# A transformer-style trunk layer: the last block of pass B gathers its expert rows instead of multiplying the whole second table

## The chip, the cores and the metric

The kernel runs on one core of a Trainium2 chip. A core has TensorE (matrix products), VectorE (DVE), ScalarE (ACT) and GpSimd (POOL), SyncE (SP) which here only issues transfers, and 16 DMA engines that all queues share. The metric is the time of one execution on the device in microseconds. The kernel before takes 2957.24 us, the median of three runs (2951.74 to 2960.56).

## The reference

x is 1024 tokens of 1024 features, eight blocks of 128 tokens, all float32.

```
h   = LN(x) * (1 + scale1) + shift1
[u, v, gB, gC, z, ga, gb] = h @ W_in
yA  = gelu(u) * (W_s . LN(gelu(v)) + b)         yB = gB * conv3(gC * z)
m   = sigmoid(ga) * (yA @ P_A) + sigmoid(gb) * (yB @ P_B)
x   = LN(alpha * x + gate1 * (m @ W_o))
h2  = LN(x) * (1 + scale2) + shift2
x   = LN(alpha * x + gate2 * PEER(h2))
```

PEER is where the change lies. Each token forms 8 queries (heads); each is scored against two sets of 128 keys; the 16 best pairs of keys name 16 of 128 x 128 = 16384 experts, with softmax gates. An expert is one row of `expert_u` and one of `expert_v` (1024 values each): the token's result is the sum over its 8 x 16 = 128 experts of gate x gelu(u_row . h2) x v_row.

## The kernel before, in words

**Two passes.** Pass A holds blocks 0 to 2, pass B blocks 3 to 7 (`NBLK`, line 39). `UNITS` (`_order`, line 54) is one list of work units that every engine goes through in the same order: the front layers of A, those of B with A's queries among them, then B's queries among its first E units, 64 E units, and 64 W units, two W units to a group. A unit is 1 MB of weights. Products are made exact enough in fp16: weights and activations are each split into a high and a low half, and three matmuls (high x high, high x low, low x high; lines 1718 to 1720) stand for one. ScalarE makes the high half of a unit's weights (`make_hi`), VectorE the low half (`make_lo`, line 1043), three or four units ahead (`NW` = 4 slots, two staging buffers).

**Pass A is sparse.** Its experts' rows are gathered: 384 slots (3 blocks x 128), for each slot one row of either table for 128 tokens at once, 4096 bytes a token. GpSimd issues one indirect transfer for a slot (line 746) once the row buffer is free (`row_used`), VectorE dots a first-table row with h2 (`u_row`, line 1139) or adds a weighted second-table row (`v_row`, line 1148). `SECTION` says how many slots of each table go beside which unit, `_places` gives each row a buffer out of the ring of its phase (`BUFFERS`: 7 buffers beside the ranking, 5 and 6 around the spreading, 9 in the main loop).

**Pass B is dense.** For all 16384 experts the E units compute gelu(u_row . h2) for the 640 tokens (96 matmuls of 320 columns a unit) and store them, `a_dram`. VectorE meanwhile ranks the scores of B head by head (`rank`). In the spread units, 20 from unit 40 on, 32 tokens a unit, the gates are spread out to a dense table of experts by tokens: VectorE builds one-hot matrices (`onehot_keys`, line 1496, `onehot_gate`, line 1503), TensorE multiplies them, ScalarE stores the result, `g_dram`. Four E units follow them.

**The main loop.** 32 groups of 512 experts. SP loads a group's activations (`A_t`) and every second time two groups' gates (`G_t`); VectorE multiplies them (`product`, line 1510), ScalarE makes the high half, VectorE the low one (`coefficients_lo`, line 1519). TensorE multiplies these coefficients with the group's second-table rows: 10 output tiles, five blocks by two halves of the features, 12 matmuls of 512 columns each. Seven tiles stay in seven banks of PSUM over all groups. The other three share the eighth bank, and VectorE adds them into SBUF after each group (`shared_out`, line 1641). Pass A's rows go on beside it: 5 or 6 slots of each table a group up to group 23, then those of the second table alone.

**The end.** When the last product is made, SP loads the residual blocks back (`x_end`), and VectorE and ScalarE close one block after another in `CLOSE_ORDER`: scale, add, layer norm, store.

The queues run in the order in which the program is written; there is no planner. On VectorE an iteration of the main loop is:

```
some(1)
make_lo(first_w + 2 * g + NW - 1)
shared_out(g, 0)
product(g + 1)
some(2)
shared_out(g, 1)
coefficients_lo(g + 1)
make_lo(first_w + 2 * g + NW)
some(2)
```

Of the kernel before, what the change touches and what calls it, by code (L numbers as in the profile page):

```python
# [175 lines left out]
X_G = X_IDX + 6  # L176
X_END = X_G + NT // 4
# [13 lines left out]
N_SPREAD = NT // 32  # L191
E_SPREAD = 2 * NGRP - N_SPREAD - 4
# [8 lines left out]
SLOTS = SB * HEADS * TOPK  # L201
LAG = 32


def _sections():
# [6 lines left out]
    for e in range(2 * NGRP):  # L212
        k["B", "E", e] = 2 + e % 2 if e < E_SPREAD - 4 else 2
# [25 lines left out]
ROW_OF = {row[:2]: m for m, row in enumerate(ROWS)}  # L239

# [4 lines left out]
           "out": [0, 1, 2, 3, 12, 13, 14, 15, 16]}  # L245
# [38 lines left out]
SHARED = ((1, 0), (4, 0), (2, 1))  # L284
OUT_ORDER = [(b, half) for half in range(2) for b in range(DB)]
# [4 lines left out]
FINISH = [((0, 0), (N_MAIN,)), ((0, 1), (N_MAIN,)), ((1, 1), (N_MAIN,)), ((0, 0), (N_MAIN + 1,)),  # L290
          ((0, 1), (N_MAIN + 1,)), ((1, 0), (N_MAIN, N_MAIN + 1)), ((1, 1), (N_MAIN + 1,))]
FINISH += [((b, half), (N_MAIN, N_MAIN + 1)) for b in range(2, DB) for half in range(2)]
FINISHED = {t: i + 1 for i, (t, _) in enumerate(FINISH)}
LAST_SHARED = [t for t, _ in FINISH if t in SHARED]
CLOSE_ORDER = [0, 1, 3, 4, 2, 5, 6, 7]
SHARED_POS = [OUT_ORDER.index(t) for t in SHARED]

# [1730 lines left out]
```

## Time and profile before

| | us |
|---|---|
| median of three runs | 2957.24 |
| span of the profiled execution, first to last instruction | 2939.3 |
| TensorE busy | 2830.0 |
| VectorE busy | 2512.5 |
| GpSimd busy | 1029.0 |
| ScalarE busy | 885.5 |

The page gives only the span of the profiled execution; the median lies 17.9 us above it. A busy share is a mean over stages with different limits. The granted clock of TensorE was 0.99 of full speed over the span. A matmul's duration in a row (381 ns for 512 columns) contains its pipeline; they start closer together than that. "Idle" in a group's row is the engine's idle time just before its instructions, with what ended it. The share of DMA is the mean over the 16 engines of the time in which packets were under way.

### The profile page before, as it was taken

How to read it: one execution, taken by the hardware profiler on the slowest of the kernel's cores; microseconds unless marked ns; L12 is line 12 of the kernel's file. 1: busy time of each engine (PE TensorE's matmuls, PEld its weight loads, DVE VectorE, ACT ScalarE, POOL GpSimd, SP SyncE). 2: the span in 40 equal slices, each digit the busy share in tenths (PEclk: the TensorE clock that was granted, in tenths of full speed). 3: DMA queues.
4: the chain of work that ended last, by engine and by line, in shares of the span. 5: the costliest groups of instructions: out<-in, count | busy, mean ns of one | idle time of the engine just before them, and what ended most of it. 6: DMA issues, size and time to landing. Idle time of an engine off the chain costs nothing. (4 is left out here: it accounts for less than half of the span.)

```text
span 2939.3 us, 47358 instructions
## 1 busy us (share of the span) xinstructions
PE 2830.0 (96%) x19184; PEld 1834.9 (62%) x19184; DVE 2512.5 (85%) x4708; ACT 885.5 (30%) x1321; POOL 1029.0 (35%) x778
## 2 busy tenths in 40 slices
PE   4999999998999999999999999999999999999998
PEld 4566686766667877677776677777544444444443
DVE  6876556987887879999999999998699999999877
ACT  3333532221111432222222344444222222222223
POOL 0000000002776025444554532222456566655410
PEclk9999999999999999999999999999999999999999
DMA  8989653433999458888888999999999999999972
GB/s 328 348 318 381 238 199 129 144 123 115 391 392 378 192 215 288 303 325 314 330 315 320 354 327 346 350 346 341 368 398 405 405 388 414 407 401 404 364 267 115
DMA packets 222971, 917.54 MB, mean 312 GB/s; under 512 B 20208, under 2 KB 61216, under 8 KB 181536
## 3 DMA queue, kind: packets, MB, share of 16 engines
q1 hardware_dynamic: 61664, 427.91, 37.3%
q0 software_dynamic: 110592, 402.70, 36.4%
q10 hardware_dynamic: 50496, 83.89, 7.9%
q8 instruction: 152, 2.49, 0.3%
q14 instruction: 67, 0.55, 0.1%
HBM read 771.79 MB, written 142.63 MB: 311 GB/s over the span
## 5 line engine op out<-in xcount | busy, mean ns | idle before, releaser
L1718 PE MATMUL psU<-hB,w 128*128 128x320 f16 (+2 forms) x3104 | 927.4, 299 | 27.4 <-ACT Z L753 15.9
L1719 PE MATMUL psU<-hB,w 128*128 128x320 f16 (+2 forms) x3104 | 927.3, 299 | 0.0
L1720 PE MATMUL psU<-hB,w 128*128 128x320 f16 (+2 forms) x3104 | 927.0, 299 | 0.0
L753 ACT ACTIVATE w<-stage 128x2048 f16<-128x2048 f32 x176 | 335.7, 1909 | 606.1 <-PE psX L1720 331.2
L1043 DVE SCALAR_TENSOR_TENSOR w<-stage,w 128x2048 f16<-128x2048 f32 x176 | 402.3, 2287 | 99.4 <-ACT w L753 99.4
L746 POOL DMA_INDIRECT rows<-in_u_rows,idx_sp x200 | 267.8, 1339 | 376.0 <-DVE rows L1139 233.5
L1718 PEld LDWEIGHTS psU<-hB,w 128*128 128x128 f16 x3104 | 304.9, 98 | 140.2 <-issue 22.9
L1720 PEld LDWEIGHTS psU<-hB,w 128*128 128x128 f16 x3104 | 305.1, 98 | 117.6
L1719 PEld LDWEIGHTS psU<-hB,w 128*128 128x128 f16 x3104 | 305.0, 98 | 110.4
L746 POOL DMA_INDIRECT rows<-in_v_rows,idx_sp x205 | 271.4, 1324 | 285.4 <-DVE rows L1139 184.5
L1718 PE MATMUL psX<-w,Z 128*128 128x512 f16 x768 | 292.2, 381 | 7.6 <-DVE Z L1641 4.2
L1719 PE MATMUL psX<-w,Z 128*128 128x512 f16 x768 | 292.6, 381 | 0.0
L1720 PE MATMUL psX<-w,Z 128*128 128x512 f16 x768 | 292.5, 381 | 0.0
L1148 DVE SCALAR_TENSOR_TENSOR acc_sp<-rows,weight_sp,acc_sp 128x1024 f32<-128x1024 f32 x205 | 258.3, 1288 | 30.5 <-DMA rows<-in_v_rows,idx_sp 26.2
L1718 PE MATMUL psU<-w,Z 128*128 128x512 f16 (+1 forms) x768 | 265.1, 345 | 5.4 <-ACT acc_sp L753 2.8
L1139 DVE SCALAR_TENSOR_TENSOR rows<-rows,h_sp 128x1024 f32<-128x1024 f32 x200 | 239.6, 1220 | 29.8 <-DMA rows<-in_u_rows,idx_sp 28.9
L1719 PE MATMUL psU<-w,Z 128*128 128x512 f16 (+1 forms) x768 | 265.1, 345 | 0.0
L1720 PE MATMUL psU<-w,Z 128*128 128x512 f16 (+1 forms) x768 | 265.0, 345 | 0.0
L753 ACT ACTIVATE R<-psU 128x320 f32<-128x320 f32 (+1 forms) x296 | 123.1, 427 | 333.6 <-PE psU L1720 333.3
L753 ACT ACTIVATE Z<-psU 128x320 f32<-128x320 f32 (+3 forms) x228 | 97.0, 445 | 383.6 <-PE psU L1720 341.6
L1718 PE MATMUL psU<-Z,w 128*128 128x384 f16 (+1 forms) x640 | 206.5, 323 | 5.6 <-DVE w L1043 5.6
L1720 PE MATMUL psU<-Z,w 128*128 128x384 f16 (+1 forms) x640 | 206.8, 323 | 0.0
(263 smaller groups left out, 4435.8 us busy)
## 6 DMA issues: line engine op xcount, KB each, us to landing
stage<-in_u_units SPq DMA_DIRECT2D x64, 1024.0 KB, 8.8
stage<-in_v_units SPq DMA_DIRECT2D x64, 1024.0 KB, 8.0
stage<-in_w_front SPq DMA_DIRECT2D x48, 1024.0 KB, 8.6
hl_dram<-w SPq DMA_DIRECT2D x48, 1024.0 KB, 6.5
w<-hl_dram SPq DMA_DIRECT2D x48, 1024.0 KB, 7.2
a_dram<-R ACTq DMA_DIRECT2D x64, 640.0 KB, 8.0
g_dram<-Z ACTq DMA_DIRECT2D x20, 2048.0 KB, 10.7
Z<-a_dram SPq DMA_DIRECT2D x32, 1280.0 KB, 11.8
```

The costliest lines, as they stand in the source:

```text
L746: pool.indirect_dma_start(row_at[r], None, u_rows if table == "u" else v_rows, bass.IndirectOffsetOnAxis(ap=idx_sp[:, slot:slot + 1], axis ...
L753: return nc.scalar.activation(dst, src, func, scale=scale)
L1043: V.scalar_tensor_tensor(w[:, n % NW, 1, :], stage[:, v % 2, :], WS, w[:, n % NW, 0, :], ALU.mult, ALU.subtract).then_inc(lo_done, 1)
L1139: V.scalar_tensor_tensor(row_at[r], row_at[r], 1.0, h2_sp[:, slot % SB, :], ALU.mult, ALU.mult, accum_out=dots[:, c % 8, j:j + 1]).then_in ...
L1148: V.scalar_tensor_tensor(dst, row_at[r], weight_sp[:, slot:slot + 1], dst, ALU.mult, ALU.add).then_inc(row_used, 1)
L1718: mm(ps, lhs[0](k), rhs[0](k), start=start and s == 0, stop=False)
L1719: mm(ps, lhs[0](k), rhs[1](k), start=False, stop=False)
L1720: last = mm(ps, lhs[1](k), rhs[0](k), start=False, stop=stop and s == n - 1)
```

## The change

The last block of pass B (block 7) still goes through the dense E units, but its second half becomes sparse like pass A: its 128 slots' activations are fetched one value a token out of `a_dram`, by an index made on VectorE (`slots_x`), and its 128 rows of the second table are gathered and added on VectorE (`x_row`). Four blocks instead of five are spread and multiplied: 16 spread units instead of 20, eight E units after them instead of four, 8 output tiles instead of 10, each in a bank of its own, so that nothing is shared. Pass A's slots are dealt out anew: 3 or 4 a unit instead of 2 or 3 in E units 0 to 35, four instead of two in units 36 to 39, two as before in spread units, five instead of two in the last eight, and three or four instead of five or six in the main loop. There the rows of the last block are put between them, from the third group on, 28 batches of four or five; the activations of a batch are fetched two groups ahead of its rows, in one piece, by GpSimd. Cut to its core:

```diff
--- before
+++ after
 NT = NTOK["B"]
 HB = NT // 2
+DV = DB - 1
+NV = DV * P
+LAST_B = NB - 1
...
-N_SPREAD = NT // 32
-E_SPREAD = 2 * NGRP - N_SPREAD - 4
+N_SPREAD = NV // 32
+E_SPREAD = 2 * NGRP - N_SPREAD - 8
...
 SLOTS = SB * HEADS * TOPK
+X_SLOTS = HEADS * TOPK
 LAG = 32
+X_LAG = 2
...
-        k["B", "E", e] = 2 + e % 2 if e < E_SPREAD - 4 else 2
+        k["B", "E", e] = 3 + e % 2 if e < E_SPREAD - 4 else 4 if e < E_SPREAD else 2 if e < E_SPREAD + N_SPREAD else 5
...
+FIRST_W = SEC_OF["B", "W", 0]
+N_BATCH = len(SEC_UNITS) - FIRST_W - X_LAG
+BATCH = [range(X_SLOTS * i // N_BATCH, X_SLOTS * (i + 1) // N_BATCH) for i in range(N_BATCH)]
+
+def batch_of(c):
+    return c - FIRST_W - X_LAG

 def _rows():
     rows = []
     for c in range(len(SEC_UNITS)):
-        rows += [("u", s, c) for s in SEC_U[c]] + [("v", s, c) for s in SEC_V[c]]
+        here = [("u", s, c) for s in SEC_U[c]] + [("v", s, c) for s in SEC_V[c]]
+        last = [("x", s, c) for s in BATCH[batch_of(c)]] if batch_of(c) >= 0 else []
+        while here or last:
+            rows += here[:1] + last[:1]
+            here, last = here[1:], last[1:]
     return rows
...
-           "out": [0, 1, 2, 3, 12, 13, 14, 15, 16]}
+           "out": [0, 1, 2, 3, 8, 9, 12, 13, 14, 15, 16]}
...
-SHARED = ((1, 0), (4, 0), (2, 1))
-OUT_ORDER = [(b, half) for half in range(2) for b in range(DB)]
+OUT_ORDER = [(b, half) for half in range(2) for b in range(DV)]
...
+FINISH = [((b, half), (g,)) for g in (N_MAIN, N_MAIN + 1) for b in range(2) for half in range(2)]
+FINISH += [((b, half), (N_MAIN, N_MAIN + 1)) for b in range(2, DV) for half in range(2)]
...
-CLOSE_ORDER = [0, 1, 3, 4, 2, 5, 6, 7]
+CLOSE_ORDER = [0, 1, 2, LAST_B, 3, 4, 5, 6]
...
-        ps_out = psU + psX[0:3]
-        ps_shared = psX[3]
+        ps_out = psU + psX
...
-        a_dram = nc.dram_tensor("a_dram", [NGRP, P, 4, NT], F32).ap()
-        g_dram = nc.dram_tensor("g_dram", [NGRP // 2, P, NT // 32, 2 * P], F32).ap()
+        a_flat = nc.dram_tensor("a_dram", [NGRP * P * 4 * NT, 1], F32).ap()
+        a_dram = a_flat.rearrange("(g p j t) o -> g p j (t o)", g=NGRP, p=P, j=4)
+        g_dram = nc.dram_tensor("g_dram", [NGRP // 2, P, NV // 32, 2 * P], F32).ap()
...
-                sp.dma_start(A_t[g % 2], a_dram[g]).then_inc(a_in[g % 2], 16)
+                sp.dma_start(A_t[g % 2], a_dram[g][:, :, 0:NV]).then_inc(a_in[g % 2], 16)
...
+            def last_activations(i):
+                if i == 0:
+                    pool.wait_ge(x_slots_ready, 1)
+                for slot in BATCH[i]:
+                    pool.indirect_dma_start(act_x[:, slot:slot + 1], None, a_flat,
+                                            bass.IndirectOffsetOnAxis(ap=at_x[:, slot:slot + 1], axis=0)
+                                            ).then_inc(act_x_in[i], 16)
...
+                if m in FIRST_ROW and 0 <= c - FIRST_W < N_BATCH:
+                    last_activations(c - FIRST_W)
                 if before is not None:
                     pool.wait_ge(row_used, before + 1)
+                at = idx_x if table == "x" else idx_sp
...
+            def x_row(slot, c):
+                r, _, uses = PLACES[ROW_OF["x", slot]]
+                dve.wait_ge(row_in[r], 16 * (uses + 1))
+                dve.wait_ge(weight_x_ready, batch_of(c) + 1)
+                if slot:
+                    dve.wait_ge(row_used, ROW_OF["x", slot - 1] + 1)
+                V.scalar_tensor_tensor(acc_x, row_at[r], weight_x[:, slot:slot + 1], acc_x, ALU.mult, ALU.add
+                                       ).then_inc(row_used, 1)
+
+            def weigh_x(i):
+                dve.wait_ge(act_x_in[i], 16 * len(BATCH[i]))
+                at = slice(BATCH[i][0], BATCH[i][-1] + 1)
+                V.tensor_tensor(weight_x[:, at], act_x[:, at], gate_x[:, at], ALU.mult).then_inc(weight_x_ready, 1)
...
+            def slots_x():
+                i1, i2, gate = (t["B"][:, DB - 1].rearrange("p h k -> p (h k)") for t in (i1_all, i2_all, s_all))
+                low = act_x.bitcast(U32)
+                step(V.scalar_tensor_tensor(weight_x, i1, float(NKEYS), i2, ALU.mult, ALU.add))
+                step(V.tensor_copy(low, i2))
...
+                step(V.tensor_scalar(gate_x, gate, WS * AS, None, ALU.mult))
+                V.tensor_copy(at_x, weight_x).then_inc(x_slots_ready, 1)
...
             for g in range(N_MAIN):
...
                 make_lo(first_w + 2 * g + NW - 1)
-                shared_out(g, 0)
                 product(g + 1)
                 some(2)
-                shared_out(g, 1)
                 coefficients_lo(g + 1)
                 make_lo(first_w + 2 * g + NW)
                 some(2)
                 if g == N_MAIN - 1:
                     product(NGRP - 1)
-                shared_out(g, 2)
...
-                for tile in OUT_ORDER:
-                    if tile in SHARED:
-                        wait(pe, v_free, shared)
-                        shared += 1
-                        out_tile(ps_shared, tile, g, True, True).then_inc(v_ready, 1)
-                    else:
-                        out_tile(ps_out[persistent.index(tile)], tile, g, g == 0, False).then_inc(v_ready, 1)
+                for i, tile in enumerate(OUT_ORDER):
+                    out_tile(ps_out[i], tile, g, g == 0, False).then_inc(v_ready, 1)
```

`CLOSE_ORDER` takes block 7 fourth, out of its own sum `acc_x`. `N_BATCH` is 28. The tiles and views of four blocks are 512 columns wide instead of 640.

## Rows read from the trace of the kernel before

**Rows 1.** The page: span, and busy time of each engine

```profile
span 2939.3 us, 47358 instructions
...
PE 2830.0 (96%) x19184; PEld 1834.9 (62%) x19184; DVE 2512.5 (85%) x4708; ACT 885.5 (30%) x1321; POOL 1029.0 (35%) x778
```

**Rows 2.** Busy time by stretch, with clock, DMA share and GB/s

```profile
core 0: us, PE busy (x) PEld busy (x) DVE busy (x) ACT busy (x) POOL busy (x), PEclk, DMA share, GB/s
1062.00:1251.30 189.30, 184.17 (x1353) 133.47 (x1351) 178.12 (x576) 54.27 (x93) 90.80 (x70) 0.99 0.79 290
1251.30:1573.00 321.70, 321.70 (x2385) 234.32 (x2384) 298.94 (x845) 93.95 (x159) 162.86 (x125) 1.00 0.87 323
1573.00:1711.20 138.20, 125.26 (x928) 90.07 (x927) 130.38 (x286) 44.83 (x74) 68.59 (x51) 0.95 0.85 322
1711.20:2036.00 324.80, 322.18 (x3044) 244.96 (x3042) 319.73 (x453) 149.24 (x267) 86.55 (x76) 1.00 0.96 346
2036.00:2090.00 54.00, 53.28 (x386) 37.45 (x385) 32.60 (x35) 17.91 (x27) 12.40 (x10) 1.00 0.98 384
...
2140.00:2707.60 567.60, 567.60 (x2631) 257.23 (x2630) 544.37 (x599) 135.01 (x88) 347.39 (x239) 1.00 1.01 403
```

**Rows 3.** Instruction groups of 2150 to 2700 us, shapes kept apart

```profile
L746 POOL DMA_INDIRECT R<-in_v_rows,idx_sp x70 | 99.4, 1420 | 39.4 <-issue 17.7 <-DVE R L1139 16.6 <-DVE acc_sp L1148 5.1
L1043 DVE SCALAR_TENSOR_TENSOR w<-stage,w 128x2048 f16<-128x2048 f32 x43 | 98.1, 2283 | 0.0
...
L1519 DVE TENSOR_TENSOR Z<-Z 128x2560 f16<-128x2560 f32 x21 | 59.1, 2813 | 0.0
...
L1641 DVE TENSOR_TENSOR Z<-psX,Z 128x512 f32<-128x512 f32 x64 | 43.7, 683 | 8.4 <-PE psX L1720 8.3
...
L1510 DVE SCALAR_TENSOR_TENSOR Z<-Z,hB 128x640 f32<-128x640 f32 x44 | 33.2, 811 | 0.0
```

**Rows 4.** DMA queues of 2150 to 2700 us: packets, MB, share of 16 engines

```profile
q0 software_dynamic: 33108, 120.58, 55.9%
q1 hardware_dynamic: 10659, 100.41, 44.3%
```

**Rows 5.** VectorE's waits of 2150 to 2700 us

```profile
DVE Z L1641 <- PE psX L1720: 8.3, 9, 1.9
DVE acc_sp L1148 <- DMA R<-in_v_rows,idx_sp: 6.9, 6, 2.5
```

**Rows 6.** VectorE in order of time, one burst of rows in an E unit

```profile
1546.49 1.22 DVE L1139 SCALAR_TENSOR_TENSOR rows<-rows,h_sp 128x1024 f32<-128x1024 f32 x1
...
1547.64 2.48 DVE L1148 SCALAR_TENSOR_TENSOR acc_sp<-rows,weight_sp,acc_sp 128x1024 f32<-128x1024 f32 x2
1550.03 0.16 DVE L1161 SCALAR_TENSOR_TENSOR weight_sp<-dots,gate_sp 128x3 f32<-128x3 f32 x1
```

**Rows 7.** Chain of waits: VectorE's weight conversions of two spread units

```profile
1733.37 2.20 DVE w L1043
...
1750.45 2.20 DVE w L1043
```

**Rows 8.** DMA issues of 1260 to 1600 us: count, KB each, us to landing

```profile
q10 hardware_dynamic: 2880, 13.11, 9.4%
...
rows<-in_v_rows,idx_sp POOLq DMA_INDIRECT x39, 8.2
rows<-in_u_rows,idx_sp POOLq DMA_INDIRECT x33, 9.0
```

**Rows 9.** GpSimd's row issues of 2150 to 2700 us: shortest, median, longest

```profile
L746 POOL DMA_INDIRECT rows<-in_u_rows,idx_sp x55: 933/1438/3044, 2149.9 to 2690.2; - x55
...
DMA to landing us min/median/max: 5.7/10.8/19.1
```

**Rows 10.** VectorE at the end, and its first wait there

```profile
2870.35 3.02 DVE L1510 SCALAR_TENSOR_TENSOR Z<-Z,hB 128x640 f32<-128x640 f32 x4
...
2887.28 1.23 DVE L1674 SCALAR_TENSOR_TENSOR Z<-acc_sp,h_sp 128x1024 f32<-128x1024 f32 x1 [4.93 <-DMA hB<-x_dram]
```

More of the change, by code:

```diff
@@ L239 @@
 ROW_OF = {row[:2]: m for m, row in enumerate(ROWS)}
+ROWS_OF = [[row[:2] for row in ROWS if row[2] == c] for c in range(len(SEC_UNITS))]
+FIRST_ROW = {m for m, row in enumerate(ROWS) if not m or ROWS[m - 1][2] != row[2]}
 BUFFERS = {"front": [0, 1, 2, 3, 4, 5, 6, 7], "own": [0, 1, 2, 3], "rank": [0, 1, 2, 3, 8, 9, 17],
            "gates": [0, 1, 2, 3, 10], "spread": [0, 1, 2, 3, 10, 11], "last": [0, 1, 2, 3, 8, 9],
-           "out": [0, 1, 2, 3, 12, 13, 14, 15, 16]}
+           "out": [0, 1, 2, 3, 8, 9, 12, 13, 14, 15, 16]}
 def _buffers_of(unit):
@@ L489, in trunk_layer @@
         row_in = [sem(f"row_in{i}") for i in range(18)]
+        act_x_in = [sem(f"act_x_in{i}") for i in range(N_BATCH)]
         end_in = sem("end_in")
@@ L828, in indices_out @@
             def indices_out(lo, hi):
-                for i in range(lo, hi):
-                    kind, (first, last) = i // 2, SPLIT["B"][i % 2]
-                    a = X_IDX + i
-                    n, at = (last - first) * P, slice(first * P, last * P)
+                for kind in range(lo, hi):
+                    a = X_IDX + kind
                     wait_x(act, a)
                     if kind < 2:
-                        pairs = slice(first * P // 2, last * P // 2)
-                        activation(keys_t16[:, pairs, kind, :], psX[a % 4][:, 0:n].rearrange("p (n t) -> p n t", t=2)
+                        activation(keys_t16[:, :, kind, :], psX[a % 4][:, 0:NV].rearrange("p (n t) -> p n t", t=2)
                                    ).then_inc(x_free[a % 4], 1)
                     else:
-                        activation(g_t[:, at], psX[a % 4][:, 0:n], ACT.Copy, GS).then_inc(x_free[a % 4], 1)
+                        activation(g_t, psX[a % 4][:, 0:NV], ACT.Copy, GS).then_inc(x_free[a % 4], 1)
             def section_gelu(n):
@@ L1177, in section @@
                         dve.wait_ge(acc_zeroed, 1)
-                for slot in SEC_V[c]:
-                    v_row(slot)
+                for table, slot in ROWS_OF[c]:
+                    if table == "u":
+                        u_row(slot, slot - SEC_U[c][0], c)
+                    elif table == "v":
+                        v_row(slot)
+                    else:
+                        x_row(slot, c)
                     yield
@@ L1480, in idx_t @@
             def idx_t():
-                for i in range(4):
-                    a = X_IDX + 5 - i
+                for a in range(X_IDX, X_G):
                     dve.wait_ge(x_free[a % 4], a // 4 + 1)
@@ L1941, in _ @@
                     pe.wait_ge(s_shift, 2)
-                    index_tiles(0, 4)
+                    index_tiles(0, 2)
             first_w = N_OF["B", "W", 0]
-            persistent = [t for t in OUT_ORDER if t not in SHARED]
             pe.wait_ge(tile_free, E_LAST)
@@ L1949, in _ @@
                 pe.wait_ge(x_free[a % 4], a // 4 + 1)
-            shared = 0
             def out_tile(ps, tile, g, first, last):
```

112 lines of the change are left out of this document (56 added, 56 removed).

## The prediction

> **What bounds the kernel now.** I read the page's busy times first. TensorE is busy 96% of the span and VectorE 85% [rows 1], so an average names no single bound, and I went on by stretches [rows 2]. Up to 1062 us nothing of this change runs. From 1251 to 1573 us (E units, pass B's first-table product with the ranking beside it) TensorE is busy all the time and VectorE 298.9 of 321.7 us: 93%. From 1711 to 2036 us (spread units) VectorE is busy 319.7 of 324.8 us, and two weight conversions a unit apart on the chain of waits stand 17.08 us apart [rows 7]: VectorE is the bound there. From 2036 to 2090 us the last four E units take 13.5 us each and VectorE is busy for only 32.6 of 54.0 us. In the main loop (2140 to 2707 us) TensorE never pauses: 567.6 us for 2631 matmuls is 0.2157 us each, 25.9 us for a group's 120. But in the same stretch VectorE is busy 96%, and the DMA share is 1.01 at 403 GB/s. So three resources stand within a few per cent of each other there, and removing work from TensorE alone tells little. VectorE's waits in it are small (8.3 us on TensorE, 6.9 us on one kind of row) [rows 5]; that only says the rows come just in time.
>
> **What the change does to each resource of a group.** TensorE: 8 output tiles instead of 10, 96 matmuls instead of 120, 96 x 0.2157 = 20.7 us, 5.2 us less. Over 32 groups that would be 166 us, the most the edit could bring.
>
> VectorE: now 544.4 us busy in 21.9 groups, 24.8 us each. Removed: three additions out of the shared bank, 3 x 0.68 = 2.05; four products of 512 instead of 640 columns, 4 x 0.81 x 0.2 = 0.65; the low halves 2048 instead of 2560 wide, 2.81 x 0.2 = 0.56 [rows 3]. Added: one multiplication of weights, 0.16. Rows: now 5.33 dotted and 5.33 added, 10.7 in all. Then, by the sections that the code lays out: groups 0 and 1 have 3 + 3 of pass A; groups 2 to 19 have 3.2 + 3.2 of pass A and 4.6 of the last block, 11.0; groups 20 to 27 have 3.2 added and 4.6 of the last block, 7.8; groups 28 and 29 about 8. So groups 2 to 19 need 24.8 - 2.05 - 0.65 - 0.56 + 0.16 + 0.3 x 1.2 = 22.1 us of VectorE.
>
> DMA engines: 120.58 MB of row gathers are 230 gathers of 0.524 MB and take 55.9% of 550 us, 1.34 us each; SP's loads take 44.3% of 550 us for 100.41 MB, 2.43 us per MB [rows 4]. Check on now: 10.7 x 1.34 + 4.72 MB x 2.43 = 25.8 us a group, what the group takes. After, SP loads 2.10 MB of weights, 1.05 of activations and 1.05 of coefficients: 10.2 us. Groups 2 to 19: 11.0 x 1.34 + 10.2 = 24.9 us. Groups 20 to 27: 7.8 x 1.34 + 10.2 = 20.7 us.
>
> The activation gathers are new: 4.6 a group, 128 descriptors of four bytes each. Nothing like them is in the trace. Below they cost next to nothing (512 bytes), above as much as a row gather with as many descriptors, 1.34 us. I take 0.2 us each, near the low end because a thousandth of the bytes moves, so 0.9 us a group: 25.8 us for groups 2 to 19 and 21.6 us for 20 to 27.
>
> GpSimd issues all of them: 11.0 + 4.6 = 15.6 a group instead of 10.7. An issue is 0.93 us at least, 1.44 us in the median and 3.04 us at worst [rows 9], and 0.30 us lies between two (17.7 us of "issue" before 70 instructions is 0.25, part of them with another wait) [rows 3]. At 1.23 us 15.6 issues take 19.2 us, at the mean of 1.42 + 0.30 they take 26.8 us. The five small gathers go out in one piece, and no freed row buffer is refilled in those 6 to 9 us. I take 26.2 us for groups 2 to 19, a little above the DMA sum and below the GpSimd one, and 21.8 us for 20 to 27.
>
> Sum of the main loop against 25.9 a group: groups 0 and 1 at TensorE's 20.7, -10; groups 2 to 19, 18 x 0.3 = +5; groups 20 to 27, 8 x -4.1 = -33; groups 28 to 31, 4 x -5.2 = -21. At the end VectorE waits for the reload of the residual blocks, which lands 14 us after the last product, and then has eight blocks to close [rows 10]; that chain does not get shorter with TensorE's last two groups, +3. In all **-56 us**. Bounds: -138 if groups 2 to 27 go at VectorE's or TensorE's pace (18 x -3.8, 8 x -5.2), -23 if GpSimd sets 28 us for groups 2 to 19.
>
> On this resource the Trainium skill (DMA: Bandwidth & Descriptors, Specifications) speaks against the change: it puts memory traffic of one core at about 358 GB/s. By that an 11-row group's 9.95 MB would take 27.8 us, 36 us more in all. The trace has 403 GB/s over 568 us, so I go by the trace.
>
> **E units 0 to 39.** The rows taken out of the main loop come here: one more of each table in units 0 to 35, two more in 36 to 39, 44 pairs. In a burst a dotted row starts 1.15 us after the last (1546.49 to 1547.64) and an added one 1.20 us (1547.64 to 1550.03 for two) [rows 6]: 2.35 a pair, 103.4 us of VectorE. Its idle time from 1062 to 1711 us is 11.2 + 22.8 + 7.8 = 41.8 us [rows 2]. Nothing of the ranking goes, as all five blocks are still ranked. If all idle time were filled, the stretch grows by 62 us; if none, by 103. I take that half stays, since part of it is waiting for other engines: **+82 us**. It can be more: bursts become 6 and 8 rows for seven buffers, so the eighth row is asked for only when the first is used, some 8 us before it is needed, and rows land 8.2 to 9.0 us after their issue [rows 8]. In units 38 and 39 eight rows share five buffers.
>
> Building the last block's indices adds a dozen small instructions on a busy VectorE, each like the 0.16 us of [rows 6], with waits between: **+3 us**.
>
> **E units 40 to 63.** Now 20 spread units of 17.08 and four of 13.5, 395.6 us. After, 16 spread units (each still spreads 32 tokens with two rows of each table, so 17.08): 273.3 us. The last eight have ten rows each. VectorE then needs 2.2 + 5 x 2.35 + 0.2 = 14.2 us, TensorE 13.0, but the DMA engines 10 x 1.34 + 1.05 x 2.43 + 0.655 MB x 2.44 (9.4% of 340 us for 13.11 MB [rows 8]) = 17.5 us, and six buffers that turn over in about 0.3 + 9 + 1.2 us give ten rows in 17.5 us too. I take 18, so 144, and 8 more for the first two groups' loads (4.2 MB), which lie today beside the four light units at a DMA share of 0.98 [rows 2]. 425 against 396: **+29 us**. Bounds: -7 (14.5 us a unit, loads hidden) to +45 (20 us).
>
> **Sum.** -56 + 82 + 3 + 29 = +58 us. The profiled execution's span is 2939.3 us; what lies around it, up to the median of 2957.2, is 17.9 us and is not touched. I predict 2957.2 + 58 = **3015 us**.
>
> **Rivals.**
> (a) The transfers are not a bound: DMA share 1.01 is a queue that is kept full, not one that limits, and GpSimd keeps up. For it speaks that TensorE never waits today. Then the main loop gives -138, the last units -7, the E units +72: 2957 - 138 - 7 + 72 + 3 = 2887 us. Against it: the sum of bytes by rate comes out at the group's very time, and the same engines do not exceed 403 GB/s over 568 us. It decides if groups 2 to 19 fall under 24 us.
> (b) The four-byte gathers cost like row gathers, 1.34 us: +6.1 us a group. Groups 2 to 19 then take 31.0 (+92), 20 to 27 take 26.8 (+7), the first two lose most of their gain, and the main loop ends at +78: 3149 us. It is the same count of descriptors that speaks for it, the bytes against it. The Trainium skill (DMA: Bandwidth & Descriptors, Specifications) leans to this side: transfers under 512 bytes are read, modified and written; but the same page's floor of 10.5 ns a packet would make it an estimate of 0.08 us a gather. No row here shows such a gather.
> (c) A wash: the E units fill all of VectorE's idle time (+62), the last eight units run at their DMA sum with the first loads hidden (+17), groups 2 to 19 at 24.9 (-18) and 20 to 27 at 20.7 (-42), -88 with the other terms: 2957 + 62 + 17 + 3 - 88 = 2951 us. Each is possible; all together need transfers without any gap, and they have gaps wherever buffers run out.
>
> **Chances.** Forecast 0.68 (its own range 2980 to 3060), (a) 0.11, (b) 0.07, (c) 0.14, spread from 2930 to 2975. A measurement here tells 0.3%, 9 us. Faster by more: (a) and a third of (c), 0.16. Within: 0.06. Slower: 0.78. The range that leaves out no more than 2 in 10 goes from 2940, into (c), to 3080, short of (b).
>
> **What would show it.** Right: VectorE over 97% busy from 1062 to about 1780 us with TensorE under 95%; spread units still 17.08; the last eight E units at 17 to 19 us with VectorE waiting for rows; groups 2 to 19 near 26 us with TensorE waiting, 20 to 27 near 22. Wrong: groups 2 to 19 at 22 to 23 us (then (a)), above 29 (then (b)), or E units with ranking that grow by less than a pair's 2.35 us minus their share of idle time.

## The result, and the profile after

The changed kernel takes 3035.17 us, the median of four runs (3026.71 to 3036.82), against 2958.03 us of the kernel before on the same chip (2951.74 to 2960.56): the ratio is 1.0262, with an interval of 1.0219 to 1.0305. It is slower, as forecast, by 77 us where 58 were predicted. Its profiled execution took 3035.97 us with a span of 3033.8 us.

The page of the changed kernel, the line of [rows 1] again:

```profile
span 3033.8 us, 45503 instructions
...
PE 2709.3 (89%) x18157; PEld 1756.4 (58%) x18157; DVE 2551.7 (84%) x4713; ACT 844.6 (28%) x1281; POOL 1298.5 (43%) x1035
```

TensorE has lost 120.7 us of work, VectorE has gained 39.2 and GpSimd's issuing 269.5. The one that was relieved is the one whose average was highest; the two others had little room where the change uses them.

To see where the time went, I cut both traces at the same pieces of work: the stores of the activations of E units 1, 38, 41, 56 and 64, and the low halves of the coefficients of groups 2, 20 and 28. The stretches of the changed kernel, in the columns of [rows 2]:

```profile
core 0: us, PE busy (x) PEld busy (x) DVE busy (x) ACT busy (x) POOL busy (x), PEclk, DMA share, GB/s
1101.30:1778.10 676.80, 596.30 (x4218) 421.67 (x4216) 629.72 (x1662) 165.18 (x288) 361.54 (x287) 0.94 0.86 323
1778.10:1864.70 86.60, 46.77 (x352) 33.62 (x350) 74.36 (x103) 16.70 (x30) 51.73 (x41) 0.76 0.87 323
1864.70:2121.10 256.40, 254.33 (x2402) 193.25 (x2400) 252.14 (x357) 117.67 (x211) 68.67 (x61) 1.00 0.97 349
2121.10:2254.70 133.60, 103.75 (x763) 74.31 (x761) 96.73 (x116) 30.16 (x50) 83.00 (x62) 0.90 0.99 375
2254.70:2319.80 65.10, 42.88 (x181) 18.53 (x182) 48.80 (x56) 9.89 (x8) 48.13 (x41) 0.80 0.92 344
2319.80:2754.60 434.80, 394.17 (x1736) 172.58 (x1734) 398.71 (x412) 103.03 (x73) 343.42 (x275) 0.95 1.03 405
2754.60:2921.40 166.80, 162.00 (x743) 72.80 (x742) 153.12 (x136) 45.25 (x28) 131.19 (x102) 0.99 1.02 402
```

The same cuts through the kernel before, for three of them:

```profile
1073.90:1658.10 584.20, 572.78 (x4204) 414.22 (x4202) 548.61 (x1559) 171.77 (x289) 293.04 (x220) 0.99 0.85 314
1658.10:1711.20 53.10, 46.45 (x369) 34.44 (x368) 47.10 (x64) 17.54 (x33) 25.22 (x20) 0.94 0.86 326
2138.40:2605.20 466.80, 466.80 (x2165) 211.49 (x2163) 448.23 (x494) 111.46 (x73) 288.47 (x197) 1.00 1.01 403
```

| stretch | before, us | after, us | difference | predicted |
|---|---|---|---|---|
| up to the first E unit's store | 1073.9 | 1101.3 | +27.4 | 0 |
| E units up to the 38th | 584.2 | 676.8 | +92.6 | } +85 |
| units 39 to 41 | 53.1 | 86.6 | +33.5 | } |
| 15 of the spread units | 256.2 | 256.4 | +0.2 | 0 |
| last eight units (4 spread, 4 light before) | 120.6 | 133.5 | +12.9 | } +19 |
| last unit to the coefficients of group 2 | 50.4 | 65.1 | +14.7 | } |
| groups 2 to 19 (25.93 us each, then 24.15) | 466.8 | 434.8 | -32 | +5 |
| groups 20 to 27 (25.76 us each, then 20.86) | 206.1 | 166.9 | -39 | -33 |
| the rest | 128.1 | 112.4 | -15.7 | -18 |

From the first store on that is +67.0 us against the predicted +58. The 27.4 us ahead of it are code that the change leaves as it was: the kernel before, profiled again, came to its first store at 1095.3 us instead of 1073.9 (run r0_before below). The profile of before was some 16 us shorter than its median: its span of 2939.3 us lies 17.9 us under it, where the spans of the other profiles lie 1.8 to 2.2 us under the time of their own execution. The profile of after stood on its median. So some 16 of the 27.4 us are luck of the one execution. What is left, 11 us, is within what twelve profiles vary there (1068 to 1101 us), and what makes it stays open.

The granted clock of TensorE is lower in the changed kernel (0.952 over the span, 0.990 before). It is the lower of its two levels (1.2 of 2.4 GHz) for short times after TensorE has waited (behind a wait of 8.04 us that ends at 2437.91 us its matmuls take 0.61 us instead of 0.38). That doesn't make TensorE the bound: in groups 2 to 19 its clock is 0.95, by which 96 matmuls of 0.2157 us are an estimate of 21.8 us against 24.15 measured, and it still waits for coefficients:

```profile
PE psU L1775 <- DVE Z L1592: 33.7, 10, 8.0
```

### The profile page after: what moved, and what is told of

It reads as the page before. It is cut to its first block, busy times and chain, and to the rows that moved or that the text cites. A ratio compares the mean times of both kernels' runs of the same rounds, so it can differ in the third digit from the quotient of the medians.

```text
span 3033.8 us, 45503 instructions
## 1 busy us (share of the span) xinstructions
PE 2709.3 (89%) x18157; PEld 1756.4 (58%) x18157; DVE 2551.7 (84%) x4713; ACT 844.6 (28%) x1281; POOL 1298.5 (43%) x1035
## 4 chain that ended last, share of the span: by engine, by line
DVE 33%; issue 20%; DMA 16%; PE 14%; POOL 14%; ACT 2%; SPq 0%; DVEq 0%; ACTq 0%; POOLq 0%
DVE acc_sp L1182 5%; DVE w L1077 5%; PE psU L1775 5%; PE psU L1776 5%; PE psU L1777 5%; POOL rows L783 5%; DMA Z<-in_v_rows,idx_sp 4%; POOL Z L760 4%; DMA rows<-in_v_rows,idx_sp 4%; POOL R L783 3%; DVE Z L1569 3%; DVE rows L1173 3%; POOL Z L783 2%; DMA stage<-in_w_front 2%; DVE Z L1576 2%
## 5 line engine op out<-in xcount | busy, mean ns | idle before, releaser
L1775 PE MATMUL psU<-hB,w 128*128 128x320 f16 (+2 forms) x3104 | 939.7, 303 | 104.1 <-ACT R L790 71.6
L1776 PE MATMUL psU<-hB,w 128*128 128x320 f16 (+2 forms) x3104 | 938.7, 303 | 7.3 <-issue 7.2
L1777 PE MATMUL psU<-hB,w 128*128 128x320 f16 (+2 forms) x3104 | 938.4, 303 | 4.0 <-issue 3.9
L1775 PEld LDWEIGHTS psU<-hB,w 128*128 128x128 f16 x3104 | 308.3, 99 | 226.7 <-issue 105.4
L783 POOL DMA_INDIRECT rows<-in_u_rows,idx_sp x200 | 245.7, 1229 | 328.9 <-DVE rows L1173 196.3
L1777 PEld LDWEIGHTS psU<-hB,w 128*128 128x128 f16 x3104 | 308.4, 99 | 132.8 <-issue 10.6
L1776 PEld LDWEIGHTS psU<-hB,w 128*128 128x128 f16 x3104 | 308.4, 99 | 128.1 <-issue 12.6
L783 POOL DMA_INDIRECT rows<-in_v_rows,idx_sp x222 | 281.6, 1268 | 214.2 <-DVE rows L1173 137.2
L1775 PE MATMUL psU<-w,Z 128*128 128x512 f16 (+1 forms) x768 | 273.4, 356 | 95.4 <-DVE Z L1592 92.4
L1182 DVE SCALAR_TENSOR_TENSOR acc_sp<-rows,weight_sp,acc_sp 128x1024 f32<-128x1024 f32 x222 | 283.5, 1294 | 53.5 <-DMA rows<-in_v_rows,idx_sp 47.1
L1173 DVE SCALAR_TENSOR_TENSOR rows<-rows,h_sp 128x1024 f32<-128x1024 f32 x200 | 238.6, 1222 | 50.1 <-DMA rows<-in_u_rows,idx_sp 37.9
L1776 PE MATMUL psU<-w,Z 128*128 128x512 f16 (+1 forms) x768 | 272.7, 355 | 0.0
L1777 PE MATMUL psU<-w,Z 128*128 128x512 f16 (+1 forms) x768 | 272.3, 355 | 0.0
L790 ACT ACTIVATE Z<-Z 128x2048 f16<-128x2048 f32 (+2 forms) x49 | 81.3, 1675 | 556.8 <-issue 236.4
L783 POOL DMA_INDIRECT Z<-in_v_rows,idx_sp x120 | 153.9, 1282 | 135.8 <-DVE Z L1173 93.0
L1775 PE MATMUL psU<-Z,w 128*128 128x384 f16 (+1 forms) x640 | 206.9, 323 | 3.9 <-DVE w L1077 3.8
L1776 PE MATMUL psU<-Z,w 128*128 128x384 f16 (+1 forms) x640 | 206.8, 323 | 0.4 <-issue 0.4
L1777 PE MATMUL psU<-Z,w 128*128 128x384 f16 (+1 forms) x640 | 206.9, 323 | 0.0
L1777 PE MATMUL psX<-w,Z 128*128 128x512 f16 x512 | 194.8, 381 | 3.1 <-issue 3.1
## 6 DMA issues: line engine op xcount, KB each, us to landing
g_dram<-Z ACTq DMA_DIRECT2D x16, 2048.0 KB, 10.5
```

The source lines that it names most:

```text
L783: pool.indirect_dma_start(row_at[r], None, u_rows if table == "u" else v_rows, bass.IndirectOffsetOnAxis(ap=at[:, slot:slot + 1], axis=0)) ...
L790: return nc.scalar.activation(dst, src, func, scale=scale)
L1173: V.scalar_tensor_tensor(row_at[r], row_at[r], 1.0, h2_sp[:, slot % SB, :], ALU.mult, ALU.mult, accum_out=dots[:, c % 8, j:j + 1]).then_in ...
L1182: V.scalar_tensor_tensor(dst, row_at[r], weight_sp[:, slot:slot + 1], dst, ALU.mult, ALU.add).then_inc(row_used, 1)
L1775: mm(ps, lhs[0](k), rhs[0](k), start=start and s == 0, stop=False)
L1776: mm(ps, lhs[0](k), rhs[1](k), start=False, stop=False)
```

## The experiments

Each ratio is to the kernel before, run on the same chip beside it. Each shortened diff shows what differs from the kernel that is named. Where totals are compared, keep in mind that the part ahead of the first E unit's store, which only the edits of e7 and e8 touch (their gathers begin at about 717 us), took 1068 to 1101 us; so the spans from that store on are given too (1932.5 us in the profile of after).

**r0_before.** The kernel before again, with no edit.

> The kernel before once more, for a second profile. In the changed kernel TensorE lost 27 us between 837 and 1010 us, in units that the change doesn't touch, with gaps of 0.6 to 2.1 us between single matmuls. Theory A (instructions arrive late there, by chance of the execution): this profile may show such gaps too, of any size. Theory B (the change causes it): none here, as in the first profile of before; the first E unit's store is issued at 1074 us again.

Measured: 2967.62 us for the profiled execution, span 2965.8; the other runs of before on that chip went from 2930.59 to 2960.59. The 400 us in mid-front of this profile, and the same 400 us of the first profile of before:

```profile
400.00:800.00 400.00, 376.81 (x2684) 268.77 (x2682) 312.98 (x1066) 90.00 (x165) 69.13 (x56) 0.96 0.48 173
```

```profile
400.00:800.00 400.00, 391.60 (x2880) 286.19 (x2878) 311.87 (x1066) 95.23 (x176) 63.63 (x52) 0.99 0.48 174
```

One code did 2684 matmuls here and 2880 there. Part of the lost time is in gaps of 0.5 to 2.5 us between single matmuls which wait for nothing that the profile shows: from 640 us to the first store 16 gaps and 14.1 us in this execution, 12 gaps and 11.4 us in the profile of after, none in the first profile of before. Another part is the granted clock, which falls to its lower level behind such gaps; 60 us of this profile, and of the first:

```profile
760.00:820.00 60.00, 48.23 (x279) 28.94 (x278) 31.72 (x47) 5.09 (x14) 30.86 (x29) 0.80 0.81 317
```

```profile
760.00:820.00 60.00, 53.52 (x385) 37.91 (x383) 48.62 (x67) 7.27 (x20) 41.56 (x36) 0.94 1.02 404
```

From the first store to the end the two profiles of before agree within 0.3% (1865.4 and 1870.5 us), so the table above can be read from there on, to some 5 us in a stretch (groups 2 to 19 took 26.23 us each in this profile), and nothing ahead of it.

**e1_before_new_deal.** The kernel before, with the changed kernel's deal of pass A's rows: the E units take 44 pairs more and the main loop 88 rows less, but the last block stays dense.

```
-  k["B", "E", e] = 2 + e % 2 if e < E_SPREAD - 4 else 2
+  k["B", "E", e] = 3 + e % 2 if e < E_SPREAD - 4 else 4 if e < E_SPREAD else 2
```

> The kernel before with one part of the change: pass A's slots dealt as 3 or 4 in E units 0 to 35 and 4 in units 36 to 39, the main loop with fewer. Theory A (VectorE sets the pace of E units 0 to 39, and its idle time there is not to be filled): 44 pairs x 2.35 = 103 us, and 10 to 15 us of waits in units 38 to 40, +115; the main loop stays at TensorE's 25.9 us a group, so 3070 us. Theory B (the idle time is filled, what the changed kernel lost comes from its other parts): +62 to +82, 3020 to 3040 us.

Measured: 3076.05 us (3070.11 to 3078.99), ratio 1.0439 (1.0386 to 1.0491). Its E units and its main loop:

```profile
1092.40:1771.10 678.70, 593.07 (x4222) 419.88 (x4220) 629.59 (x1663) 164.39 (x288) 359.93 (x288) 0.94 0.87 323
2276.10:2742.30 466.20, 466.20 (x2162) 211.37 (x2160) 388.71 (x415) 112.62 (x73) 177.29 (x146) 1.00 0.92 351
```

The E units take what they take in the changed kernel (678.7 and 676.8 us), so the deal alone makes this term, and neither the indices nor anything else of the last block. The main loop stays at 25.9 us a group although VectorE has 59.5 us less to do than in the same groups of before (448.2 down to 388.7) and the DMA share falls from 1.01 to 0.92. So TensorE did bind the kernel before; the others were a few per cent behind.

**e2_after_gate_units_light.** The changed kernel, with two rows of each table instead of four in units 36 to 39. In the last two of these only five buffers are to be had.

```
-  ... else 4 if e < E_SPREAD else 2 if e < E_SPREAD + N_SPREAD else 5
+  ... else 2 if e < E_SPREAD + N_SPREAD else 5
```

> The changed kernel with two slots instead of four in E units 36 to 39; the eight pairs go to the main loop. Theory A (eight rows on five buffers make VectorE wait for rows there): the stretch from the 38th to the 41st store falls from 86.6 us by 31 (8 x 2.35 and 12 of waits), the main loop grows by 16 x 1.34 = 21 us, 3025 us. Theory B (the length comes from the last block's indices and the start of the spreading): it falls by 19, 3037 us.

Measured: 3027.13 us (3017.74 to 3028.35), ratio 1.0269 (1.0216 to 1.0321). The stretch from the 38th to the 41st store:

```profile
1774.20:1834.00 59.80, 45.51 (x355) 33.44 (x354) 54.81 (x79) 16.75 (x30) 29.68 (x24) 0.87 0.86 324
```

It gives 26.8 us back, 19.6 us of them VectorE's work (74.4 to 54.8) and 7.2 us its idle time (12.2 to 5.0). The total hardly moves: the eight pairs go to the main loop, where groups 2 to 19 rise from 24.15 to 25.05 us (+16) and groups 20 to 27 from 20.86 to 21.33 (+4). From the first store on it is 1928.0 us against 1932.5. A row costs about the same in either place.

**e3_after_old_deal.** The changed kernel with the old deal: all 44 pairs go back to the main loop.

```
-  k["B", "E", e] = 3 + e % 2 if e < E_SPREAD - 4 else 4 if e < E_SPREAD else ...
+  k["B", "E", e] = 2 + e % 2 if e < E_SPREAD - 4 else ...
```

> The changed kernel with the old deal in E units 0 to 39 (2 or 3, and 2); all 44 pairs go back to the main loop. Theory A (the main loop is bound by the transfers, 1.34 us a row): the E units lose 115 us, the main loop gains 88 x 1.34 = 118, about 3037 us, no better. Theory B (the main loop is bound by VectorE, or has room): at 44 x 2.35 on top of 22.1 us in 20 to 28 groups it grows by less, 40 to 75 us, 2960 to 2995 us.

Measured: 3038.38 us, ratio 1.0317 (1.0236 to 1.0398). Three of the four runs lie between 3021.1 and 3050.8 us, with a median of 3026.0; one took 4684.74 us at a granted clock of 0.56 instead of 0.95, which I can't explain and which nothing here rests on. Its main loop, groups 2 to 19:

```profile
2175.30:2698.30 523.00, 403.25 (x1728) 174.50 (x1728) 462.98 (x493) 102.94 (x73) 413.55 (x327) 0.89 1.01 391
```

The E units are back at 574.4 us, and the groups go up to 29.05 and 25.82 us: 18 x 4.9 + 8 x 5.0 = 128 us more in the loop against 137.6 us less in units 1 to 41. GpSimd makes 327 issues of 1.265 us with 0.30 us after each, 511.7 of the 523.0 us. The deal of the rows is a wash (1926.5 us from the first store on, against 1932.5); what costs is that the changed kernel has the last block's second-table rows and as many small gathers on top.

**e4_no_activation_gathers.** The changed kernel without the four-byte gathers.

```
-  for slot in BATCH[i]:
-      pool.indirect_dma_start(act_x[:, slot:slot + 1], None, a_flat, ...)
...
-  dve.wait_ge(act_x_in[i], 16 * len(BATCH[i]))
```

> The changed kernel without the 128 four-byte gathers of activations (the weights of the last block's rows are then made from other values). In the changed kernel groups 2 to 19 took 24.2 us each. Theory A (GpSimd's issues bind: 275 issues x 1.25 + 0.30 us fill 427 of 435 us): without 4.6 issues a group 7 us of GpSimd go, and the groups fall to VectorE's 22.1 us, the kernel to about 2995 us. Theory B (the DMA engines bind with the bytes of the rows, the small gathers are free on both): 24.0 us a group, 3030 us. Theory C (a four-byte gather holds the DMA engines like a row): 6 us a group less for the DMA engines, which also ends at 22.1 us.

**e5_small_loads.** The changed kernel with the gathers, but SP loads only a quarter of a group's activations from group 2 on, and a sixteenth of the gates from group 4 on.

```
-  sp.dma_start(A_t[g % 2], a_dram[g][:, :, 0:NV])
+  sp.dma_start(A_t[g % 2][:, 0, 0:NV], a_dram[g][:, 0, 0:NV])
...
-  sp.dma_start(G_t[pair % 2] ..., g_dram[pair])
+  sp.dma_start(G_t[pair % 2][:, 0:1] ..., g_dram[pair][:, 0:1])
```

> The changed kernel, but from group 2 on SP loads only a quarter of a group's activations and a sixteenth of its gates (the products then use old values): 1.8 MB a group less, 4.5 us of the DMA engines. Theory A (GpSimd binds): groups 2 to 19 stay near 24 us. Theory B (the DMA engines bind): they fall to VectorE's 22.1 us. If both stand at the same height, 23 to 23.5 us.

**e6_no_gathers_small_loads.** Both edits in one kernel.

> Both of the last two in one kernel: neither the small gathers nor the full loads. Whichever of GpSimd and the DMA engines binds, it is freed: groups 2 to 19 at VectorE's 22.1 us, 20 to 27 at TensorE's 20.7 us, the kernel at about 2990 us. If the groups stay above 23.5 us, what binds is neither (the waits between VectorE and TensorE for the low halves).

Measured, with the main loop of each:

| kernel | median us | ratio (interval) | groups 2 to 19 | 20 to 27 |
|---|---|---|---|---|
| after | 3035.17 | 1.0262 (1.0219 to 1.0305) | 24.15 | 20.86 |
| e4 | 3010.59 | 1.0185 (1.0167 to 1.0203) | 23.69 | 21.01 |
| e5 | 3009.99 | 1.0204 (1.0160 to 1.0248) | 23.68 | 20.56 |
| e6 | 2961.36 | 1.0012 (0.9992 to 1.0032) | 21.96 | 19.79 |

From the first store on the profiles of e4, e5 and e6 took 1916.8, 1917.5 and 1874.2 us: 16, 15 and 58 us less than that of after. What their medians gained beyond that (25, 25 and 74 us in all) lies ahead of it, where nothing was edited.

Stretches of the main loop of e4, of e5, and of e6:

```profile
2300.00:2700.00 400.00, 364.27 (x1635) 160.97 (x1632) 370.96 (x382) 94.72 (x67) 237.54 (x181) 0.96 1.02 411
```

```profile
2300.00:2700.00 400.00, 367.77 (x1652) 162.75 (x1649) 374.16 (x385) 95.59 (x68) 323.16 (x253) 0.97 0.91 336
```

```profile
2300.00:2660.00 360.00, 348.38 (x1608) 156.36 (x1607) 359.32 (x372) 93.75 (x66) 219.39 (x175) 1.00 0.98 370
```

This is the picture of two limits side by side. Without the small gathers GpSimd is free (237.5 us and 181 gaps of 0.3 us make 292 of 400), the DMA share stays at 1.02, and a group gains 0.46 us. Without the bytes the share falls to 0.91, GpSimd is full (323.2 + 253 x 0.3 = 399 of 400), and a group gains 0.47 us. Only with both gone is the next limit reached, and it is VectorE, busy 359.3 of 360.0 us: 21.96 us a group, where the prediction's working had 22.1 for VectorE. A group's time is taken at VectorE's low halves, which can catch up by a group; so the 19.79 us of groups 20 to 27 can lie below TensorE's 20.7. I had expected 2990 us for e6, 29 more than it took; the groups were as expected, so most of the miss is elsewhere: half of it ahead of the first store (1086.3 us against 1101.3), some of it in the first loads (55.1 us from unit 64 to group 2, against 65.1).

In e4 GpSimd waits for row buffers that VectorE has to free. One kind of these waits comes to 96.3 us in the 400 us; in groups 2 to 19 of after all of them made 8.1 us:

```profile
POOL R L779 <- DVE Z L1200: 96.3, 31, 5.1
```

**e7_after_half_rows and e8_before_half_rows.** The kernel after, and the kernel before, with 2048 instead of 4096 bytes gathered for each token and slot; all engines do as much work as with whole rows. The dotted rows are multiplied by zero, so the results are not those of the layer.

```
-  pool.indirect_dma_start(row_at[r], None, u_rows if table == "u" else v_rows, ...)
+  pool.indirect_dma_start(row_at[r][:, 0:512], None, half_rows, ...)
```

> The changed kernel with row gathers of 2048 instead of 4096 bytes a token, at the same count; VectorE works on 1024 columns as before (the other half of a buffer is multiplied by nothing). Theory A (E units 0 to 39 are bound by VectorE's work, and about 35 us of 677 by rows that land late): from the first to the 38th store 640 to 650 us instead of 676.8, and 38th to 41st 75 instead of 86.6 us. Theory B (its idle time there has other causes): no change. Last eight E units: from the 56th to the 64th store 120 instead of 133.5 us. Groups 2 to 19: at VectorE's 22.1 us if the DMA engines bind, near 24 us if GpSimd does.

> The kernel before with row gathers of 2048 instead of 4096 bytes a token, everything else as it is. In the changed kernel this brought 77 us. Theory A (the kernel before is bound by TensorE in the E units and the main loop, by VectorE in the spread units, its transfers only just keep up): the main loop stays at 25.9 us a group, the E units change by less than 5 us, 2950 us in all. Theory B (the transfers bind the main loop before too): its groups fall under 25 us.

Measured: e7 2958.05 us, ratio 1.0001 (0.9988 to 1.0014); e8 2907.36 us, ratio 0.9885 (0.9859 to 0.9910). The E units up to the 38th of e7, then those and the main loop of e8:

```profile
1077.50:1731.30 653.80, 585.01 (x4210) 417.37 (x4208) 628.08 (x1660) 165.21 (x288) 361.94 (x286) 0.95 0.66 221
```

```profile
1068.30:1636.10 567.80, 567.80 (x4204) 412.85 (x4202) 552.05 (x1564) 173.77 (x289) 274.49 (x221) 1.00 0.67 226
2120.00:2680.00 560.00, 560.00 (x2596) 253.81 (x2595) 539.12 (x592) 134.56 (x86) 331.91 (x233) 1.00 0.80 295
```

In e7 groups 2 to 19 stay at 24.15 us with a DMA share near 0.8:

```profile
2250.70:2685.40 434.70, 395.27 (x1747) 173.41 (x1745) 398.75 (x410) 101.77 (x73) 352.13 (x272) 0.96 0.81 288
```

GpSimd alone holds them there: 352.1 + 272 x 0.3 = 433.7 of 434.7 us. That it is the very time of after is chance, as an issue took 1.295 us here and 1.249 there. The gain of e7 is in the E units (-23.0 us) and in the stretches after them (the last eight units take 119.0 instead of 133.5 us), 49 us from the first store on. The rest of the 77 us by which its median is lower lies ahead of that store (1077.5 us instead of 1101.3); no run tells whether the bytes of the rows gathered there have a part in them. In e8 the main loop stays at 25.79 us a group, as expected of a kernel bound by TensorE. I missed the size of the rest: the E units gave 16.4 us, the gate units 6.9 and the handover to the main loop 6.7. So the bytes of the rows already cost the kernel before some 30 us around the E units, which no average of the DMA share (0.85) tells.

**e10_no_last_block.** The changed kernel with nothing of the second table for the last block: neither its gathers nor its added rows, while the product is still 8 tiles.

```
-  BATCH = [range(X_SLOTS * i // N_BATCH, X_SLOTS * (i + 1) // N_BATCH) for i in range(N_BATCH)]
+  BATCH = [range(0) for i in range(N_BATCH)]
...
-  if batch_of(c) >= 0: weigh_x(batch_of(c))
```

> The changed kernel without the last block's second half: neither its activation gathers nor its 128 rows, nor the work on them. Theory A (the last block's sparse path costs what it holds of the queues): groups 2 to 19 are left with 6.4 rows, 18.8 us of the DMA engines, 12 us of GpSimd and 16 of VectorE, so TensorE's 20.7 us bind; 27 us less of E units do not come back. The kernel about 3035 - 18 x 3.4 - 5 = 2965 us, no faster than before although it computes less. Theory B (the new waits between VectorE and TensorE hold the groups, whatever the rows): above 22 us a group.

Measured: 2932.43 us, ratio 0.9971 (0.9959 to 0.9984). A stretch of its main loop:

```profile
2250.00:2600.00 350.00, 346.40 (x1605) 156.71 (x1604) 290.40 (x304) 96.50 (x66) 164.32 (x118) 1.00 0.98 378
```

Groups 2 to 19 take 20.2 us and groups 20 to 27 take 20.73; TensorE binds. The total is lower than I expected, by some 30 us. This profile came to its first store at 1074.6 us instead of 1101.3, which is most of that; from there on it took 1856.2 us, where the kernel before took 1865.4 and 1870.5. The run is a bound for the whole idea: with the E units dealt as they are now, even a last block that costs nothing would gain 0.3% on the kernel before.

No version run here is both complete and faster than the kernel before. Three things were not tried: one indirect transfer that fetches the activations of several slots, E units with more buffers, and a deal between the old and the new one.

## Why the prediction was right, and where its sizes were wrong

The direction and its reason held: three resources stood within a few per cent of each other, and the change takes work from one of them and gives it to the other two and to GpSimd. But that the sum is so close (+67.0 against +58) is luck: two errors of some 40 us cancel. Of its own signs of being right, the spread units (17.09 us) held; VectorE was to be over 97% busy up to 1780 us and was 93%, groups 2 to 19 were to be near 26 us and the last eight E units at 17 to 19 us, and they were at 24.15 and 16.7.

**E units 0 to 39: the mis-sized term.** Predicted +85 with the indices, measured 92.6 + 33.5 = +126.1. The work was right: VectorE is busy 108.4 us more (81.1 and 27.3), and 44 pairs of 2.35 us and the indices make 106. What failed is the step "I take that half stays" for the idle time. Nothing of it was filled; it grew, from 35.6 to 47.1 us up to unit 38 and from 6.0 to 12.2 us after that. VectorE of the changed kernel, in order of time, in one unit beside the ranking:

```profile
1482.76 1.23 DVE L1173 SCALAR_TENSOR_TENSOR rows<-rows,h_sp 128x1024 f32<-128x1024 f32 x1 [0.29 <-DMA rows<-in_u_rows,idx_sp]
...
1488.55 1.22 DVE L1173 SCALAR_TENSOR_TENSOR rows<-rows,h_sp 128x1024 f32<-128x1024 f32 x1 [4.56 <-DMA rows<-in_u_rows,idx_sp]
...
1492.48 1.23 DVE L1173 SCALAR_TENSOR_TENSOR rows<-rows,h_sp 128x1024 f32<-128x1024 f32 x1 [2.70 <-DMA rows<-in_u_rows,idx_sp]
...
1494.27 3.84 DVE L1182 SCALAR_TENSOR_TENSOR acc_sp<-Z,weight_sp,acc_sp 128x1024 f32<-128x1024 f32 x3 [0.55 <-DMA Z<-in_v_rows,idx_sp]
```

and the DMA engines around it:

```profile
1485.00:1500.00 15.00, 12.55 (x81) 8.34 (x79) 8.20 (x9) 3.31 (x6) 6.37 (x6) 0.89 1.02 417
```

VectorE stands idle for nearly half of these 15 us because the rows it is to work on are not there, while the DMA engines are full at 417 GB/s. The mean share of the stretch is 0.86. The waits for rows make most of the idle time, in the changed kernel 33.7 of 47.1 us (the four lines below) and in the kernel before 24.1 of 35.6:

```profile
DVE acc_sp L1182 <- DMA Z<-in_v_rows,idx_sp: 10.9, 4, 4.7
DVE acc_sp L1182 <- DMA rows<-in_v_rows,idx_sp: 9.5, 6, 3.3
DVE rows L1173 <- DMA rows<-in_u_rows,idx_sp: 7.5, 3, 4.6
DVE Z L1173 <- DMA Z<-in_u_rows,idx_sp: 5.8, 2, 3.7
```

Time spent waiting for rows can't be filled with more rows. With half the bytes the waits for rows fall to 15.3 us in e7 and to 0.4 in e8, and the idle time to 25.7 and 15.8. My warning on units 38 and 39 (eight rows, five buffers) was right in kind: idle time there doubles. Which share of the waits is due to the buffers and which to the bytes beyond these runs stays open.

**The main loop, groups 2 to 19.** Predicted 26.2 us, measured 24.15; 18 groups make 37 us. The failed step is "I take 0.2 us each" for the four-byte gathers on the DMA engines, and the margin put on GpSimd. The DMA queues of the 434.8 us, in the columns of [rows 4]:

```profile
q0 software_dynamic: 30263, 101.15, 59.1%
q1 hardware_dynamic: 15865, 74.83, 43.3%
```

Queue 0 moved 101.15 MB, 193 row gathers, in 59.1% of 434.8 = 257 us: 1.33 us each, where [rows 4] gave 1.34, with the 81 small gathers in the same 257 us. Of these 257 us the packets of 4096 bytes took 253.2, and the smaller ones that the trace has 3.9, so a small gather costs the DMA engines about 0.05 us instead of 0.2. On GpSimd each costs an issue like any other:

```profile
L760 POOL DMA_INDIRECT Z<-a_dram,Z x81: 940/1897/2016, 2332.5 to 2753.5; - x81
```

and GpSimd's idle time in this stretch is the 0.3 us between two issues, hardly ever a wait for a buffer:

```profile
POOL R L783 <- issue: 26.9, 83, 1.8
...
POOL Z L760 <- issue: 24.7, 81, 0.3
...
POOL R L783 <- DVE Z L1204: 5.3, 4, 2.9
```

275 issues of 1.249 us and 0.30 us each make 426 of 434.8 us. The mean of an issue was lower than the 1.42 us that I took from [rows 3]. So GpSimd and the DMA engines bind together, the first at 23.7 and the second at 24.7 by its shares, which reach 1.03. The mechanism, an issue's price on GpSimd beside the bytes on the DMA engines, was in the prediction; both came out smaller.

The chain of waits shows how it looks when GpSimd sets the pace, with five small gathers in one piece:

```profile
2405.84 1.68 POOL R L783
2407.52 0.31 issue
2407.82 1.92 POOL Z L760
2409.74 0.30 issue
2410.04 1.90 POOL Z L760
2411.95 0.30 issue
2412.25 2.02 POOL Z L760
...
2417.15 1.78 POOL R L783
```

**Groups 20 to 27** at 20.86 us: predicted 21.8. The DMA sum of 21.6 less the 0.9 that the small gathers don't cost is 20.7, but TensorE's 96 matmuls make 20.7 too, and e10, bound by TensorE, has 20.73 there. e4 has 21.01 and e5 20.56. Which of the two binds these groups stays open.

**Units 40 to 63 and the handover.** The spread units are 17.09 us apart as [rows 7] has them (predicted 17.08). Of the last eight units and the first loads I expected +29, and -10 from groups 0 and 1; together the trace has 0.2 + 12.9 + 14.7 = +27.8 against +19. Up to the store of unit 64 the units cost less than thought (133.5 us), and the handover more: TensorE is busy 42.9 of 65.1 us there. Groups 0 and 1 did not run at TensorE's pace.

**The rivals.** (a), the transfers are no bound: refuted by its own point of decision, groups at 24.15 and not under 24 us, though narrowly, and by e5, where fewer bytes bring 0.47 us a group, and e6. Yet half of its ground was true, as TensorE did bind the kernel before (e1, e8). (b), small gathers priced like row gathers on the DMA engines: refuted by queue 0. Its estimate of 0.08 us a gather spreads 128 packets of 10.5 ns over 16 engines. The Trainium skill (DMA: Bandwidth & Descriptors, Measured) gives that floor as the time of a whole transfer of 64 packets over their number, so by it 128 packets would be an estimate of 1.34 us, the price of (b). The trace has 0.05 us. (c), the wash: its loop was near (24.9 and 20.7 expected, 24.15 and 20.86 measured), but it needed the idle time of the E units filled, and the opposite happened.

The Trainium skill (DMA: Bandwidth & Descriptors, Specifications) puts memory traffic of one core at about 358 GB/s, half of what a stack gives its two cores. By that 175.98 MB would need 492 us; the trace has them in 434.8 us at 405 GB/s, so for this kernel, which runs on one core, that half is no limit and the measurement decides.

## What to carry to other kernels

When several resources are within a few per cent of each other, write down what each needs after the change, work and issue slots alike; relief for one is worth only the distance to the next (here 25.9 to 24.15 us a group, not to 20.7). Idle time that an engine spends waiting for data is no room for more work on data of the same kind: look at what ends it before counting on it. And when taking away either of two costs gives little, take away both in one run before calling them harmless: from the first store on e4 gave 16 us, e5 15 us, both together 58.

## What the runs showed of the hardware that I had not expected

**A gather of four bytes a partition** costs the DMA engines about 0.05 us (above) and GpSimd no less than one of 4096 bytes: 0.94 us at least, where those have 0.93. In groups 2 to 19 the mean is 1.49 us for the 81 small ones and 1.16 us for the 193 others, because the small ones go out in one piece beside VectorE's low halves more often (next point).

**An issue stretches beside VectorE.** An indirect transfer's issue takes 0.93 us, but when it starts while VectorE makes a weight's low half it ends only after that. So it was for all 35 such issues of groups 2 to 19, which end 0.81 to 0.83 us after the low half, and for the 18 that started in a low half of coefficients. GpSimd and VectorE of the changed kernel in order of time:

```profile
2437.78 2.28 DVE L1077 SCALAR_TENSOR_TENSOR w<-stage,w 128x2048 f16<-128x2048 f32 x1
2438.97 1.90 POOL L760 DMA_INDIRECT Z<-a_dram,Z  x1 [0.30 <-issue]
...
2441.18 0.95 POOL L783 DMA_INDIRECT R<-in_u_rows,idx_sp  x1 [0.30 <-issue]
```

The low half ends at 2440.06, the issue at 2440.87, 0.81 us after it; the next issue starts together with the dot of a row (L1173) and takes 0.95 us. Beside such shorter instructions issues took 0.93 to 2.02 us. The Trainium skill (SBUF — State Buffer, Who interferes with whom) says that a VectorE instruction with two inputs in SBUF contends with a GpSimd instruction that reads SBUF, and that the ports they share are locked for one of them. The same section of the Trainium skill infers that making descriptors needs only the write side, by which these issues would not wait. The trace agrees with the first and speaks against the second, as the issues end behind both kinds of low half; the other way round no stretch was seen (the 36 low halves of the loop take 2.28 us in the mean, [rows 3] has 2.28).

**Matmuls that wait for nothing shown.** Some executions reach the first E unit's store 21 to 27 us later than the first profile of before (1095.3 and 1101.3 against 1073.9 us), with 11 to 14 us in gaps of 0.5 to 2.5 us between matmuls, between about 730 and 985 us, and a granted clock at the lower level behind them. One such place in the profile of after, TensorE alone:

```profile
846.29 0.10 PEld L1776 LDWEIGHTS psU<-hB,w 128*128 128x128 f16 x1 [1.74 <-issue]
846.31 0.44 PE L1776 MATMUL psU<-hB,w 128*128 128x320 f16 x1 [0.99 <-issue]
```

Packets of the instruction queue q8 lie far apart there: 37 us in r0_before (773 to 810 us) and 32 us in after (826 to 858), against 13 to 22 us in the first profile of before. Late loading of instructions would fit, but the packets may as well come late because TensorE was held up; no run here took it away, so it is argued, not shown.
